# First weight's first part loaded between the two tiles of x, its products made token tile by token tile, on one core of a Trainium2 chip

## The reference

```python
def reference(x, ...):
    for i in range(DEPTH):                      # 2
        if i % 2 == 0:
            mix = moba_attention(x, ...)        # starts with proj = x @ w_in, w_in 1024 x 3072
        else:
            mix = nsa_attention(x, ...)
        x = layer_norm(DEEPNORM_ALPHA * x + mix, ln_g[i, 0], ln_b[i, 0])
        ffn = grouped_moe(x, router_w, router_b, moe_w_gate[i], moe_w_up[i], moe_w_down[i])
        x = layer_norm(DEEPNORM_ALPHA * x + ffn, ln_g[i, 1], ln_b[i, 1])
    return x
```

## Time and profile before

| | us |
|---|---|
| runs (three) | 1209.30, 1209.31, 1207.87 |
| median | 1209.3 |
| the profiled execution's own time | 1207.55 |
| its span, first to last instruction | 1205.7 |
| mean granted TensorE clock | 0.935 |

### The profile page before, as it was taken

The page is one execution under the profiler, slowest core; times in us unless marked ns, Lnnn a source line. Parts: engine busy times, 40 slices in busy tenths (PEclk is TensorE's granted clock), DMA queues, the critical chain, the costliest instruction groups (busy, mean ns, idle before and its releaser), DMA issues.

```text
span 1205.7 us, 18281 instructions
## 1 busy us (share of the span) xinstructions
PE 1021.0 (85%) x7610; PEld 565.5 (47%) x7610; DVE 310.5 (26%) x866; ACT 183.4 (15%) x473; POOL 43.3 (4%) x109
## 2 busy tenths in 40 slices
PE   9999999976698975668899999999967798876766
PEld 7586544443343532343678655544523433432432
DVE  2435521321111111111221785403211111111112
ACT  1024210110010000000221563201100010100002
POOL 1001010000000000000100120100000000000000
PEclk9999999998899988889999999999987899978888
DMA  9955899999999999999995308999999999999995
GB/s 354 364 210 192 341 373 418 427 427 427 427 428 428 426 425 429 428 428 422 368 352 214 137 1 316 357 422 425 426 427 428 426 426 428 428 426 428 427 426 236
DMA packets 56851, 449.05 MB, mean 372 GB/s; under 512 B 4643, under 2 KB 11044, under 8 KB 29628
## 3 DMA queue, kind: packets, MB, share of 16 engines
q1 hardware_dynamic: 54752, 442.52, 89.1%
q0 software_dynamic: 1680, 4.88, 1.1%
q10 hardware_dynamic: 332, 0.42, 0.1%
HBM read 446.72 MB, written 1.07 MB: 371 GB/s over the span
## 4 chain that ended last, share of the span: by engine, by line
PE 52%; DMA 42%; DVE 2%; ACT 1%; issue 1%; SPq 1%; DVEq 0%
DMA ring<-in_moe_w_down 16%; PE bank L1010 14%; DMA ring<-in_moe_w_up 11%; DMA ring<-in_moe_w_gate 10%; PE bank L779 7%; DMA bias<-in_moe_w_up 5%; PE bank L857 4%; PE bank L968 4%; PE bank L1074 3%; PE bank L1050 2%; PE bank L1224 2%; PE bank L1089 2%; PE bank L1331 1%; PE bank L1321 1%; PE bank L1061 1%; PE bank L1250 1%
## 5 line engine op out<-in xcount | busy, mean ns | idle before, releaser
L1010 PE MATMUL bank<-ring,work 128*32 128x256 f32 (+1 forms) x2656 | 323.6, 473 | 106.6 <-DMA ring<-in_moe_w_up 36.8
L1010 PEld LDWEIGHTS bank<-ring,work 128*32 128x32 f32 (+1 forms) x2656 | 151.9, 130 | 233.1 <-issue 201.8
L1635 DVE TENSOR_TENSOR work<-work,bank 128x256 f32<-128x256 f32 (+1 forms) x32 | 15.6, 487 | 526.0 <-PE bank L1010 526.0
L1074 PE MATMUL bank<-ring,work 128*32 128x512 f32 x576 | 99.3, 658 | 13.0 <-DMA ring<-in_moe_w_down 8.0
L1010 PE MATMUL bank<-softmax_area,work 128*32 128x256 f32 (+1 forms) x352 | 65.3, 499 | 32.8 <-DMA ring<-in_moe_w_gate 22.2
L779 PE MATMUL bank<-xT,ring 128*128 128x256 f32 x384 | 85.7, 382 | 1.1 <-ACT acc L482 1.1
L1648 DVE TENSOR_TENSOR xs<-xs,bank 128x512 f32<-128x512 f32 x112 | 71.0, 682 | 41.4 <-PE bank L1092 23.2
L779 PEld LDWEIGHTS bank<-xT,ring 128*128 128x128 f32 x384 | 72.1, 190 | 13.3 <-issue 3.8
L1010 PE MATMUL bank<-bias,work 128*32 128x256 f32 (+1 forms) x384 | 77.6, 485 | 0.0
L968 PE MATMUL bank<-work,acc 128*128 128x128 f32 (+1 forms) x448 | 75.5, 323 | 0.0
L968 PEld LDWEIGHTS bank<-work,acc 128*128 128x128 f32 x448 | 66.0, 191 | 16.6 <-issue 11.5
(11 more groups left out here) (286 smaller groups left out, 1128.3 us busy)
## 6 DMA issues: line engine op xcount, KB each, us to landing
ring<-in_moe_w_gate SPq DMA_DIRECT2D x44, 2048.0 KB, 28.7
ring<-in_moe_w_up SPq DMA_DIRECT2D x40, 2048.0 KB, 30.0
ring<-in_moe_w_down SPq DMA_DIRECT2D x36, 2048.0 KB, 29.2
softmax_area<-in_moe_w_down SPq DMA_DIRECT2D x8, 2048.0 KB, 25.8
bias<-in_moe_w_gate SPq DMA_DIRECT2D x6, 2048.0 KB, 33.1
softmax_area<-in_moe_w_up SPq DMA_DIRECT2D x6, 2048.0 KB, 28.5
bias<-in_moe_w_up SPq DMA_DIRECT2D x6, 2048.0 KB, 28.8
bias<-in_moe_w_down SPq DMA_DIRECT2D x6, 2048.0 KB, 33.3
```

The costliest lines, as they stand in the source:

```text
L1010: last = mm(bank[2 + k][row:row + cap, 0:width], xgT_of(group_of[i])[:, t, at + e * cap:at + (e + 1) * cap], w[e](t)[:, part * width:(part ...
L1074: last = mm(bank[5][row:row + CAP_NARROW, :], hidT_narrow[:, m, CAP_NARROW * e:CAP_NARROW * (e + 1)], w[e](m)[:, n * 512:(n + 1) * 512], s ...
```

## The change

SP issues the weight's first part between the two tiles of x. PE makes the first part's products for 128 tokens at a time: after the transposes of tile 0 and the two small products it waits for tile 0's copies and the weight, makes the products of column tiles 0 and 1 with tile 0, then waits for tile 1 of x and transposes it, makes column tiles 2 and 3 with tile 0, waits for tile 1's copies, and makes all four column tiles with tile 1. The second part's products are as before.

```diff
+            def load_first_part(k):
+
+                a, b = FIRST_PARTS[k]
+                src = moba_uses[0]
+                sp.dma_start(ring[:, 0, :].rearrange("p (t n) -> p t n", t=KT)[:, a:b, :], src[:, a:b, :]).then_inc(first_loaded[k], 16)
+
             for tt in range(NT):
                 sp.dma_start(xs[:, tt, :], x_in[0, tt * P:(tt + 1) * P, :]).then_inc(x_loaded[tt], 16)
+                load_first_part(tt)
...
-                        continue
-                    for k, (a, b) in enumerate(FIRST_PARTS):
-                        sp.dma_start(ring[:, 0, :].rearrange("p (t n) -> p t n", t=KT)[:, a:b, :], src[:, a:b, :]).then_inc(first_loaded[k], 16)
...
-            for tt in range(NT):
+            def transpose_first(tt):
+
                 pe.wait_ge(x_loaded[tt], 16)
                 for half in range(2):
                     for t in range(4):
                         last = tr(bank[FIRST_BANKS[tt] + half][:, t * P:(t + 1) * P], xs[:, tt, 4 * half + t::KT], ident)
                     last.then_inc(xT_ready, 1)
-            mm(bank[6][:, 0:P], blank[:, 0:P], blank[:, 0:P], start=True, stop=True)
-            mm(bank[6][:, 0:P], blank[:, 0:P], blank[:, 0:P], start=True, stop=True)
-            xT_here(0, NT - 1)
...
-                def part(m, t):
-                    return mm(bank[m // 2][:, (m % 2) * SEQ:(m % 2 + 1) * SEQ], tile_cols(m)(w, t), xT[:, t, :],
-                              start=(t == 0 and m % 2 == 0), stop=(t == KT - 1 and m % 2 == 1))
+                def part(m, t, tokens=slice(0, SEQ)):
+                    at = m % 2 * SEQ
+                    return mm(bank[m // 2][:, at + tokens.start:at + tokens.stop], tile_cols(m)(w, t), xT[:, t, tokens],
+                              start=(t == 0 and m % 2 == 0 and tokens.start == 0), stop=(t == KT - 1 and m % 2 == 1))
+
+                def first_depths(tt, tiles):
+                    for t in range(*FIRST_PARTS[0]):
+                        for m in tiles:
+                            part(m, t, slice(tt * P, (tt + 1) * P))
+
+                transpose_first(0)
+                for _ in range(2):
+                    mm(bank[6][:, 0:P], blank[:, 0:P], blank[:, 0:P], start=True, stop=True)
+                xT_here(0, 0)
                 pe.wait_ge(first_loaded[0], 16)
-                for t in range(*FIRST_PARTS[0]):
-                    for m in range(4):
-                        part(m, t)
+                first_depths(0, (0, 1))
+                transpose_first(1)
+                first_depths(0, (2, 3))
+                xT_here(0, 1)
+                first_depths(1, range(4))
                 pe.wait_ge(first_loaded[1], 16)
```

## The result

| | before | after |
|---|---|---|
| median of 6 runs, us | 1209.3 (1207.87 to 1209.73) | 1213.82 (1212.90 to 1214.66) |
| profiled execution, us | 1207.55 | 1213.79 |
| its span, us | 1205.7 | 1212.0 |
| mean granted clock | 0.935 | 0.926 |

The ratio is 1.0038, 95% interval 1.0028 to 1.0049. The prediction was 1209.1, in a range to 1210.8.

What follows compares the result with a forecast made beforehand. PE's gapless chain from the weight's landing to routing was taken as the bound; 7.03 start + 5.37 products + 0.88 transposes + 0.1 waits = 13.38 against 13.55, 0.2 us earlier, so 1209.1 us, range 1207.0 to 1210.8.

Steps and rivals of the forecast that it cites:

- The transfers: Head's loads: weight's first part lands at 6.9 instead of 8.24, tile 1 at about 8.2, second part still at 12.5.
- The start: First products in the head start at 7.03 instead of 8.37, after DVE's copy of tile 0 ends: 1.34 us earlier.
- The short products and transposes: Head's first part: 48 instructions cost 5.37 us, 0.19 more than before; tile 1's transposes add 0.88 us to the path.
- the rule on overlap: Weight loads overlap products only on other array rows; for 24 added loads an estimated 2.6 us, not 0.19; disbelieved from the trace.
- the two waits: Head's waits for tile 1 of x and for its copies: both hidden, but 0.05 us bubble each, 0.1 in all.
- The gain of the head: Head's first part ends at 13.38 against 13.55: 0.17 us earlier, say 0.2.
- the sum: Head's first part: 7.03 + 5.37 + 0.88 + 0.1 = 13.38, against 13.55.
- The clock rival: Clock rises 1 us later in the head, 5 steps longer by 0.1: +0.3 net, 1209.6; chance 0.08.
- so a shift passes through the full DMA stage at its own size: Experts' stage behind the head: transfers are released by events, so the head's shift arrives neither multiplied nor swallowed.
- there tile 1 had to be waited for: Why layer 1's head's 0.45 us PE idle wasn't taken as the wait's price; kept only in the range.
- The rivals: Late weight in the head (0.22), late clock rise (0.08), weight loads bounding short products (0.03), downstream shift (0.09).
- downstream: Unforeseen shift of more than 0.2% in the experts' stages, either direction; chance 0.09, of it 0.04 slower.

Runs made afterwards that it cites:

- b_dead48: Kernel before plus 24 transposes (48 real instructions) on PE in layer 0's overflow path, which isn't taken; 1213.84 us, ratio 1.0042.
- b_dead160: Kernel before plus 80 transposes (160 instructions) on PE in layer 0's overflow path, which isn't taken; 1207.97 us, ratio 0.9989.
- b_swap: Kernel before with only SP's new order of issue (weight's first part between the tiles of x), PE unchanged; 1212.15 us in one run.
- a_peonly: Changed kernel with SP's old order of issue, PE's new order kept, and 104 transposes in the path not taken; 1208.82 us in one run.
- b_dead24: Kernel before plus 12 transposes (24 instructions) on PE in layer 0's overflow path, which isn't taken; 1210.80 us, ratio 1.0007.
- b_pad160: Kernel before plus 160 no-operations in the overflow path not taken, which left nothing in PE's program; ratio 0.9995.
- b_pad48: Kernel before plus 48 no-operations in the overflow path not taken, which left nothing in PE's program; ratio 0.9997.
- a_nobranch: Changed kernel without PE's part of layer 0's overflow path, so without a PE branch between the layers; 1207.39 us, ratio 0.9979.
- b_wait48: Kernel before plus 48 executed instructions, waits already met, ahead of layer 0's gate products; 1214.09 us, ratio 1.0045.
- a_pad208: Changed kernel plus 208 no-operations in the overflow path not taken, which left nothing in PE's program; ratio 1.0032.
- a_pad112: Changed kernel plus 112 no-operations in the overflow path not taken, which left nothing in PE's program; ratio 1.0043.
- a_run208: Changed kernel plus 208 no-operations where PE executes, ahead of layer 0's gate products; they left nothing in the program; ratio 1.0034.
- a_dead208: Changed kernel plus 104 transposes (208 instructions) on PE in layer 0's overflow path, which isn't taken; 1209.43 us, ratio 1.0005.
- a_dead112: Changed kernel plus 56 transposes (112 instructions) on PE in layer 0's overflow path, which isn't taken; 1208.82 us, ratio 0.9999.
- b_run48: Kernel before plus 48 no-operations where PE executes, ahead of layer 0's gate products; they left nothing in the program; ratio 1.0004.
- a_wait208: Changed kernel plus 208 executed instructions, waits already met, ahead of layer 0's gate products; 1209.03 us, ratio 1.0000.

## Why the prediction was wrong, point by point

- **The transfers.** Right: weight at 6.9 (6.9 worked out), tile 1 at 8.3 (8.2). The second part came at 11.6 instead of 12.5. The prediction had expected that of ACT's later table loads, but in b_dead48 and b_dead160, where they go out as early as before (6.8 us), it landed at 11.4: the profile of before had a late landing. It was worth nothing, as said.
- **The start.** 7.20 for 7.03: the copy of tile 0 started at 6.45, not 6.24. Most of this was the clock, which rose at 5.9 us instead of 5.5 (below).
- **The short products and transposes.** Right, by their sum: from the first product to line 1282 it is 22.34 - 7.20 = 15.14 us, and before it was 22.43 - 8.37 = 14.06, a difference of 1.08 where 0.19 + 0.88 = 1.07 was reckoned for them. So the short products with their loads keep the step of the earlier trace rows, the rule on overlap of the Trainium skill ("TensorE: Matmul & The Clock Gate", part 3) doesn't hold for them, and the two waits cost nothing that can be seen, instead of 0.1.
- **The gain of the head.** 0.2 forecast, 0.07 in the pair of profiles. All the profiles say it better. In the eight with the old head (before and the kernels named b_, but for b_swap) line 1267 starts at 22.05 to 22.80, median 22.12; in the eight with the new one (all but a_peonly) it, or what it has become, starts at 22.01 to 22.72, median 22.24. The head is worth nothing that these profiles can tell; the profile of before had a weight that landed late (8.24, against 7.97 and 8.02 in b_dead160 and a_peonly), and the sum, which took that one landing for the usual one, was too kind.
- **The clock rival.** It was seen and is real. The clock's rise came at any time from 4.4 to 7.3 us in these profiles. Two with the old head, b_dead24 and then b_dead160:

```profile
4.85 3.17 PE bank L1205 x16
...
8.79 14.08 PE bank L1252 x64
```

```profile
4.86 2.31 PE L1205 MATMUL bank<-tab,xs 128*128 128x128 f32 x16
...
8.11 14.05 PE bank L1252 x64
```

With the late rise the same 16 transposes took 0.9 us more, and DVE's copy, not the weight, started the products. All of it is tenths of a microsecond.

- **The step that failed** is the one in the first part: "so a shift passes through the full DMA stage at its own size". As far as the time shift goes nothing large happened in that stage: the changed kernel was 0.07 us early at 142.95 and 0.32 us late at 579 us (579.24 against 578.92), and two profiles of what is one program differ by more (b_pad160 is 1 us behind b_pad48 there). But the change shifted something else too, the code, and the working had no term for it: 48 added instructions were costed by their 0.19 us alone, and what showed in place of nothing was 5.6 us in layer 1's head. The row that should have raised it was quoted: the 0.45 us at "issue" between two equal products. The prediction said of it that "there tile 1 had to be waited for". It hadn't; the hole is between products 15 and 16 of tile 0, two instructions ahead of that wait, and in the changed kernel it moved by as many instructions as had been added 7000 PE instructions earlier, which no wait would do.
- **The rivals.** None was it. What happened fell into the rest for "downstream" (0.09, of it 0.04 for slower), which named no mechanism.

## What to carry to other kernels

A branch in an engine's program splits it: count the instructions that a change adds or takes away ahead of it, by matmuls and weight loads, and look behind every branch for an "issue" idle between two equal instructions: here that was where the next block was waited for. If a change moves such a hole into worse cover, its time measures the placement and not the idea; shift the code by filler that isn't executed, and compare at equal places modulo 256. And see in the number of instructions of the trace, or in the fetches, that the filler is there: no-operations weren't.

## What the runs showed of the hardware

- Behind a taken branch on PE, with the DMA engines full, the first instructions came after 0.91 to 1.11 us, and where PE had to wait for the second block it went on 6.7 to 7.0 us after it had run out ahead of the branch, wherever the boundary lay: 586.44 to 593.36 before, 586.75 to 593.72 after, 586.91 to 593.86 in b_dead24, 587.49 to 594.29 in b_dead48. The hole is that time less the work that fits in. The end of a hole is fixed and its start moves by 0.056 us for each instruction. The block's fetch starts 6.1 to 6.3 us after the one before it and takes 1.0 to 1.1; why it starts so late wasn't tried.
- Without a branch no such hole was seen in the same place (a_nobranch).
- A hole of 1.78 us left the clock at its upper level. Holes of 2.90 to 3.17 us came with the lower one, from within the hole or soon behind it, in all six kernels that have them (after, b_dead48, b_wait48, a_pad208, a_pad112, a_run208); but in a_dead208, a_dead112 and b_swap it fell there without a hole. What decides it stays open.

| code behind the branch, shifted by | kernels | ratio to before |
|---|---|---|
| 0 (no filler in the program, or 256) | b_pad48, b_pad160, b_run48, a_dead208, a_wait208 | 0.9995 to 1.0005 |
| 24 | b_dead24 | 1.0007 |
| 48 | the changed one, a_pad208, a_pad112, a_run208, b_dead48, b_wait48 | 1.0032 to 1.0045 |
| 160 | a_dead112, b_dead160 | 0.9999, 0.9989 |
| no branch | a_nobranch | 0.9979 |
